# The last gathers of a mixture-of-experts layer: four roots between the gathers on GpSimd, and a norm ahead of the third addition on VectorE

## What is computed

```
h = h + mixed @ w_out[i]
u = rmsnorm(h, norm_ffn[i])
h = h + hier_moe(u, ...)          # each token: weight1 * expert_a(u) + weight2 * expert_b(u)
return rmsnorm(h, norm_final)[:, N_META:]

def rmsnorm(x, g):
    y = xf * lax.rsqrt(jnp.mean(xf * xf, axis=-1, keepdims=True) + NORM_EPS)
    return (y * g.astype(jnp.float32)).astype(x.dtype)
```

## Time and profile before

| | |
|---|---|
| median of 3 runs | 1376.61 us (1374.58 to 1378.02) |
| profiled execution | 1378.91 us, of it span 1376.7 us |
| busy share of the span | PE 95%, DVE 75%, ACT 52%, POOL 41% |
| granted TensorE clock, mean | 0.977 |

### The profile page before, as it was taken

One profiled execution on the slowest core, in us unless ns is written; L12 is line 12 of the kernel. 1 busy time (PEld: TensorE's weight loads), 2 busy tenths in 40 slices (PEclk: granted clock), 3 DMA queues, 4 the chain that ended last, 5 costly groups with the idle time before them and its releaser, 6 DMA issues. The chain is left out here.

```text
span 1376.7 us, 23896 instructions
## 1 busy us (share of the span) xinstructions
PE 1304.9 (95%) x9830; PEld 1128.8 (82%) x9830; DVE 1029.6 (75%) x1148; ACT 721.3 (52%) x826; POOL 570.4 (41%) x209
## 2 busy tenths in 40 slices
PE   5999999999999879999998799999999999999994
PEld 5999999999999768888875688888888888888871
DVE  6356566599887165666675799998998997777775
ACT  5434424212432253333423477777777777887753
POOL 1011011000000041111111687779778779999984
PEclk8999999999999989999999999999999999999998
DMA  6135655863334796555635999999999999999978
GB/s 232 42 128 154 187 184 162 243 212 107 123 93 111 242 281 184 186 170 174 199 107 173 412 425 400 404 414 411 418 406 413 398 412 408 414 417 410 401 289 320
DMA packets 142405, 374.07 MB, mean 272 GB/s; under 512 B 28368, under 2 KB 95952, under 8 KB 130016
## 3 DMA queue, kind: packets, MB, share of 16 engines
q1 hardware_dynamic: 130368, 329.87, 65.1%
q0 software_dynamic: 6912, 25.17, 5.1%
q10 hardware_dynamic: 5040, 17.83, 3.2%
HBM read 299.67 MB, written 73.17 MB: 271 GB/s over the span
## 5 line engine op out<-in xcount | busy, mean ns | idle before, releaser
L1218 PE MATMUL ps<-u_hi,w_hi 128*128 128x352 f32 (+1 forms) x720 | 239.8, 333 | 5.0 <-DVE u_lo L873 4.9
L1218 PE MATMUL ps<-u_lo,w_hi 128*128 128x352 f32 (+1 forms) x720 | 235.5, 327 | 0.0
L1218 PE MATMUL ps<-u_hi,w_lo 128*128 128x352 f32 (+1 forms) x720 | 234.6, 326 | 0.0
L2859 POOL TENSOR_TENSOR down_lo<-down_raw,down_hi 128x1024 fp32r<-128x1024 f32 x30 | 145.3, 4842 | 61.1 <-ACT down_hi L2928 61.1
L3019 DVE TENSOR_TENSOR down_lo<-down_raw,down_hi 128x3072 fp32r<-128x3072 f32 (+1 forms) x31 | 125.3, 4042 | 42.4 <-ACT down_hi L2928 42.4
L1218 PEld LDWEIGHTS ps<-u_hi,w_hi 128*128 128x128 f32 x720 | 139.1, 193 | 10.3 <-issue 5.9
L1218 PEld LDWEIGHTS ps<-u_lo,w_hi 128*128 128x128 f32 x720 | 139.0, 193 | 0.0
L1218 PEld LDWEIGHTS ps<-u_hi,w_lo 128*128 128x128 f32 x720 | 138.9, 193 | 0.0
L1658 POOL TENSOR_TENSOR mix_stat<-mix_stat,minus_half 128x4 f32<-128x4 f32 x8 | 10.7, 1335 | 299.2 <-DVE mix_stat L2037 299.2
L2928 ACT ACTIVATE down_hi<-down_raw 128x4096 fp32r<-128x4096 f32 x31 | 112.7, 3636 | 19.9 <-ACT y_out L2949 19.9
L3248 PE MATMUL ps<-first_up_hi,x_hi 128*128 128x512 f32 x256 | 103.5, 404 | 4.6 <-DVE up_lo L3019 3.3
(11 more groups left out here) (469 smaller groups left out, 3289.8 us busy)
## 6 DMA issues: line engine op xcount, KB each, us to landing
down_raw<-in_moe_w_down SPq DMA_DIRECT2D x32, 2048.0 KB, 10.6
second_gate_raw<-in_moe_w_gate SPq DMA_DIRECT2D x16, 2048.0 KB, 10.3
second_up_raw<-in_moe_w_up SPq DMA_DIRECT2D x16, 2048.0 KB, 9.4
gate_raw<-in_moe_w_gate SPq DMA_DIRECT2D x15, 2048.0 KB, 10.1
up_raw<-in_moe_w_up SPq DMA_DIRECT2D x15, 2048.0 KB, 9.3
tm_rows<-tm_stage SPq DMA_DIRECT2D x32, 512.0 KB, 4.1
y_slots<-y_out ACTq DMA_DIRECT2D x31, 512.0 KB, 11.5
w_raw<-in_w_in SPq DMA_DIRECT2D x30, 512.0 KB, 4.7
```

The costliest lines, as they stand in the source:

```text
L1218: mm = pe.matmul(z_of(n, r_), w[n % 3][:, k_, :], a[:, k_, c0:c1], start=(k_ == 0 and i == 0), stop=(k_ == KD - 1 and i == 2))
L2859: pool.tensor_tensor(lo[e % 2][:, cut:, :], raw[e % 2][:, cut:, :], hi[:, cut:, :].bitcast(F32), ALU.subtract).then_inc(sem(f"{name}_lo2_r ...
```

## The change

GpSimd makes the first four roots in between: after gather 4 comes root 0, after gather 5 root 1, after gather 6 root 2, after gather 7 root 3, and then roots 4 to 7. VectorE does norm 0 before addition 4, and addition 7 after norm 2 and no longer after norm 1. What is computed stays the same.

```
                     for t in range(NTR):
                         bring_y(t)
-                    for t in range(NTR):
+                        if t >= NTR // 2:
+                            root(t - NTR // 2)
+                    for t in range(NTR // 2, NTR):
                         root(t)
...
-                    for t in (0, 2, 4):
+                    for t in (0, 2):
                         add_rows(t)
                     for t in range(NTR):
                         last_norm(t)
-                        if t == 1:
+                        if t == 0:
+                            add_rows(4)
+                        if t == 2:
                             add_rows(7)
```

## The result

The changed kernel is slower. Over 20 runs its median is 1381.28 us (1377.24 to 1388.55), that of the kernel before 1376.48 us (1370.52 to 1382.20); the ratio is 1.0033, with a 95% interval of 1.0020 to 1.0047, which is +4.5 us (2.8 to 6.5). The forecast was +1.3 us and "no change"; its range ended at 1381.0, just under the measured time.

The account below looks back on a forecast made before the run. The start of addition 7, plus VectorE's work behind it, was taken to set the end. Addition 7 at 1367.43 against break-even 1366.14 (one norm, 1.20 us, gained) gave +1.3 us: 1377.9 us from 1376.61, range 1375.5 to 1381.0.

Parts of the forecast that it names:

- The frame: Last 30 us: the start of addition 7, plus what VectorE still has behind it, sets the end.
- the 1.20 us of gain: VectorE behind addition 7: five norms stand there instead of six, 1.20 us less.
- I take 4.57: From GpSimd's end of gather 7 to addition 7: 4.57 us as before, so addition 7 starts at 1367.43.
- the upper end, 4.71: Longest distance taken from gather's end on GpSimd to its addition, gather 2's; it would put addition 7 at 1367.57.
- gather 7 is through at 1362.86: GpSimd, with roots 0 to 2 between gathers: its last gather ends 2.49 us later than before.
- whose issue doesn't move: Additions 2 and 4 on VectorE start by gathers 2 and 4, issued as before, so no change there.
- rival A: Gathers 6 and 7 held on GpSimd by VectorE operations; addition 7 at 1368.4 to 1369.5, +2.3 to +3.4; 27%.
- Everything else is at nothing: Additions 2 and 4 unmoved, and norm 0 over 0.55 us before addition 4 wants VectorE; no cost.
- B: Gather 5 held on GpSimd through addition 2 and norm 0; addition 7 at 1370.2 to 1370.3, +4.1 to +4.2; 8%.
- C: Last gather lands sooner, 3.3 us from GpSimd to addition 7 at 1366.14; both kernels equal, 1376.6; 12%.

Follow-up runs that it names:

- the stores held: Changed kernel with SyncE holding all stores until gather 7 has landed; median 1378.11 us, ratio 1.0012 to the kernel before.
- the second execution: The changed kernel run once more, unaltered, for a second trace; 1381.35 us, ratio 1.0039 to the kernel before.
- the run with the first store held: Changed kernel with only its first store held until gather 4 has landed; 1380.17 us, ratio 1.0038 to the kernel before.
- GpSimd's half alone: Kernel before with only GpSimd's new order of roots and gathers, VectorE in its old order; median 1383.26 us, ratio 1.0040.
- one root: Changed kernel's VectorE order, but on GpSimd only root 0 ahead of gathers, behind gather 5; 1377.15 us, ratio 1.0004 to the kernel before.

## Why the prediction was wrong, point by point

*The frame held.* The start of addition 7 and what stands behind it set the end. One norm less is behind it; from addition 7 to the last norm's end it is 7.25 us, and 3.2 us on to the end of the span. So the 1.20 us of gain were there in full, and addition 7 had to start later than forecast by the whole of the error: +20.58 in place of +17.59 (1367.43 on the old clock), 2.99 us.

*The step that failed first: "I take 4.57, the row of the same gather, since the stores of norms 1 and 2 and gather 6 are under way beside it".* But in that row no store ran beside most of the gather: the first store of the kernel before was issued only at 1363.21, 2.8 us behind the end of gather 7 on GpSimd and 1.7 us ahead of addition 7, and nothing in the row shows what two earlier stores do. Measured were 6.27 and 6.79 us, and 4.28 with the stores held. This term was short by 1.70 us, and the upper end, 4.71, was no bound.

*The second: "gather 7 is through at 1362.86", 2.49 us later than before.* It was 3.78 us (and 3.97 in the second execution), 1.29 more. About 0.75 is from addition 4. The prediction had it start at +10.23, by gather 4, "whose issue doesn't move". The issue didn't; the landing did, by two microseconds, wherever the store of norm 0 was issued at about that time, and the late addition then held gather 7 on GpSimd. That was rival A's mechanism, at gather 7 only, and for a reason that A didn't have. The other 0.5 us is a later result of tile 1 (root 1 at +9.78, not +9.45) and a longer root (0.88 us, not 0.65). The result was later since TensorE's product of tile 1 took 2.55 us and not 1.95; the granted clock had fallen towards the lower level, 1.2 GHz (0.58 in the mean of 1358 to 1360), after TensorE had idled for 3.40 us. In the second execution it took 1.95 us, and root 1 started at +9.29. The two terms, 1.70 and 1.29, make the forecast's +1.3 into +4.3, against +4.2 in the traces.

*"Everything else is at nothing"* therefore missed the one thing that the moved norms also issue: their stores. I followed VectorE's norms into idle time of VectorE and not into the queue of the DMA engines. Writing down what a moved step issues would have shown it: from 1351.80 to 1364.90 the DMA engines of the kernel before were 90% busy, at 329 GB/s.

*The rivals.* B gave +4.1 to +4.2, which is what the traces measured, but by luck: its mechanism (gather 5 held through two operations back to back) falls. In the changed kernel gather 5 wasn't held at all (1.00 us), and in the run with the first store held, where it was, gather 5 started inside addition 2, which ended at 1357.14, and was over at 1358.02, in the middle of norm 0:

```profile
1356.04 1.98 POOL L2907 DMA_INDIRECT y_upper<-y_slots,slots  x1 [0.19 <-issue]
```

```profile
1355.86 1.28 DVE L3219 SCALAR_TENSOR_TENSOR h_last<-y_upper,lower_weight,h_last 128x1024 f32<-128x1024 f32 x1 [2.09 <-DMA y_upper<-y_slots,slots]
1357.07 1.28 DVE L3225 SCALAR_TENSOR_TENSOR y_upper<-h_last,rms,norm_final_rows 128x1024 f32<-128x1024 f32 x1
```

C (3.3 us from GpSimd to addition 7) did not occur for gather 7; 4.28 is its shortest. Its idea isn't refuted, though: with the stores held, gather 6, issued when little else was under way, landed 3.4 us behind its end on GpSimd. The Trainium skill ("SBUF — State Buffer", "Who interferes with whom") infers that operations with two SBUF inputs don't hold a gather: the measurement decides against it, with 1.69, 1.97 and 1.98 us for gathers that start well inside an addition and 0.99 for those that don't.

*The chances.* Since the forecast of no change rested on +1.3 with an upper end of +3.4 for A, slower by over 0.3% got 0.12. The measured ratio, 1.0033, is just above that bound, and its interval reaches down to 1.0020.

*What stays open.* No run shows how an early store delays a gather, and why mostly in one to three of its 16 parts. Two extra stores in the kernel before cost addition 7 much less than two or three stores cost it in the changed kernel. The order of issue is the likely reason and wasn't isolated. Both GpSimd's later issue and the early stores are in the +4.5 us: with GpSimd's half alone the loss is there in full, and with the stores held about a third of it is left by the ratio. How much is due to each can't be split: with the first store held, issue came 1.2 us earlier and the landing didn't, so the two overlap. Each distance is from one or two executions, with half a microsecond of scatter between two of the same kernel.

## What to carry to other kernels

When a step is moved into an engine's idle time, follow everything that it issues as well: here norms that cost VectorE nothing put 512 KB stores ahead of the gather on which the end depends, into a stretch in which the DMA engines were some 90% busy. A latency read from a trace is the latency in that company; before it is used in a sum, look at which transfers were under way beside it and which will be. And a root of half a microsecond between two DMA issues costs mostly what it waits for: GpSimd stood 1.52 us ahead of root 1 for ScalarE, and behind that for TensorE, for an operation of 0.88.

## What the runs showed of the hardware

- Stores of 512 KB took longer to land beside gathers: 4.3 to 5.9 us in the changed kernel, against 2.6 to 2.8 us for those after the last gather. A gather took 4.6 to 6.1 us from its issue in the kernel before, up to 8.0 in the changed one and 8.7 in its second execution.
- A gather that starts on GpSimd inside an addition of VectorE ends 0.81 to 0.88 us after that addition, and a start 0.12 us into a norm was enough (one root: norm 0 from 1356.14, gather 7 from 1356.26, 1.97 us). 0.05 us into one was not the earlier trace rows, nor 0.08 or 0.09 us in four other traces; in those four the VectorE operation took 1.33 or 1.34 us, where the other additions and norms of upper rows took 1.27 to 1.29. A second such operation straight behind the first adds nothing. A norm that reads PSUM didn't hold a gather (GpSimd's half alone: gather 7 from 1363.70, 0.68 us into norm 1, 0.99 us).
- A gather follows a root after 0.18 or 0.19 us on GpSimd, against 0.30 or 0.31 between two gathers.
